# Seven products for two gate and up pairs in each of seven FFNs of a two-block transformer kernel

## The reference

```
def swiglu(x, w_gate, w_up, w_down):
    return (jax.nn.silu(x @ w_gate) * (x @ w_up)) @ w_down      # 1024 -> 2816 -> 1024
```

## Time and profile before

| | us |
|---|---|
| median of 3 runs (2456.72 to 2456.9) | 2456.76 |
| span of the profiled execution | 2455.0 |
| TensorE busy | 2426.3 |
| VectorE busy | 1559.7 |
| ScalarE busy | 1183.0 |
| GpSimd busy | 205.5 |

### The profile page before, as it was taken

One profiled execution on the slowest core, in us unless ns is written; L12 is line 12 of the kernel. 1 busy time (PEld: TensorE's weight loads), 2 busy tenths in 40 slices (PEclk: granted clock), 3 DMA queues, 4 the chain that ended last, 5 costly groups with the idle time before them and its releaser, 6 DMA issues.

```text
span 2455.0 us, 30703 instructions
## 1 busy us (share of the span) xinstructions
PE 2426.3 (99%) x12690; PEld 2069.7 (84%) x12690; DVE 1559.7 (64%) x1629; ACT 1183.0 (48%) x1276; POOL 205.5 (8%) x358
## 2 busy tenths in 40 slices
PE   8999999999999999999999999999999999999998
PEld 6889998888889988888889878888888898788887
DVE  6555876655656776565558657656665677577664
ACT  5435544434437544444435664544344356644442
POOL 0100200100100101101100010011011000100010
PEclk9999999999999999999999999999999999999999
DMA  8755447657654447657664445476576454454762
GB/s 334 238 209 189 156 165 246 227 209 237 236 204 181 164 148 272 227 205 259 227 214 174 161 154 206 180 262 231 202 256 231 172 184 152 150 208 159 256 232 101
DMA packets 82547, 504.42 MB, mean 205 GB/s; under 512 B 11608, under 2 KB 12760, under 8 KB 30184
## 3 DMA queue, kind: packets, MB, share of 16 engines
q1 hardware_dynamic: 61488, 433.23, 49.2%
q0 software_dynamic: 19744, 67.65, 8.6%
q10 hardware_dynamic: 1176, 1.58, 0.4%
HBM read 476.72 MB, written 25.69 MB: 205 GB/s over the span
## 4 chain that ended last, share of the span: by engine, by line
PE 91%; DVE 5%; ACT 3%; issue 1%; DMA 1%; SPq 0%; POOL 0%; DVEq 0%; POOLq 0%; ACTq 0%
PE acc L615 24%; PE acc L616 24%; PE acc L617 24%; PE acc L583 4%; PE acc L584 4%; PE acc L585 4%; DVE w_lo L516 2%; PE aux L799 1%; ACT w_hi L508 1%; DMA raw<-in_w 1%; ACT tmp L1484 1%; PE stat L633 1%; PE bc L633 0%; PE aux L1170 0%; PE aux L981 0%
## 5 line engine op out<-in xcount | busy, mean ns | idle before, releaser
L516 DVE TENSOR_TENSOR w_lo<-raw,w_hi 128x2048 fp32r<-128x2048 f32 (+1 forms) x417 | 934.3, 2244 | 672.3 <-ACT w_hi L508 671.5
L508 ACT ACTIVATE w_hi<-raw 128x2048 fp32r<-128x2048 f32 (+1 forms) x417 | 782.8, 1880 | 624.2 <-PE acc L617 594.0
L615 PE MATMUL acc<-w_hi,x_hi 128*128 128x512 f32 (+1 forms) x1848 | 720.4, 390 | 3.1 <-DVE x_lo L1736 2.1
L617 PE MATMUL acc<-w_lo,x_hi 128*128 128x512 f32 (+1 forms) x1848 | 715.6, 387 | 0.0
L616 PE MATMUL acc<-w_hi,x_lo 128*128 128x512 f32 (+1 forms) x1848 | 715.5, 387 | 0.0
L615 PEld LDWEIGHTS acc<-w_hi,x_hi 128*128 128x128 f32 x1848 | 347.1, 188 | 77.8 <-issue 6.1
L617 PEld LDWEIGHTS acc<-w_lo,x_hi 128*128 128x128 f32 x1848 | 347.0, 188 | 71.3
L616 PEld LDWEIGHTS acc<-w_hi,x_lo 128*128 128x128 f32 x1848 | 347.2, 188 | 70.4 <-issue 1.0
L615 PE MATMUL acc<-w_hi,h_parts 128*128 128x512 f32 x704 | 274.5, 390 | 0.0
L617 PE MATMUL acc<-w_lo,h_parts 128*128 128x512 f32 x704 | 273.9, 389 | 0.0
L616 PE MATMUL acc<-w_hi,h_parts 128*128 128x512 f32 x704 | 273.9, 389 | 0.0
(11 more groups left out here) (396 smaller groups left out, 2229.3 us busy)
## 6 DMA issues: line engine op xcount, KB each, us to landing
raw<-in_w SPq DMA_DIRECT2D x399, 1024.0 KB, 4.8
squares<-tmp POOLq DMA_DIRECT2D x40, 512.0 KB, 2.9
tmp<-squares POOLq DMA_DIRECT2D x160, 128.0 KB, 4.5
raw<-in_w SPq DMA_DIRECT2D x18, 512.0 KB, 3.6
tmp<-in_norm_gb POOLq DMA_DIRECT2D x8, 1024.0 KB, 5.4
tmp<-in_norm_gb POOLq DMA_DIRECT2D x6, 512.0 KB, 3.7
tmp<-in_gate_rows POOLq DMA_DIRECT2D x12, 256.0 KB, 3.1
squares<-tmp POOLq DMA_DIRECT2D x8, 256.0 KB, 2.3
```

The lines of the kernel that those rows point to most:

```text
L508: nc.scalar.activation(w_hi[:, slot, 0:kind], raw[:, slot, 0:kind], ACT.Copy).then_inc(hi_done, 1)
L516: nc.vector.tensor_tensor(w_lo[:, slot, 0:kind], raw[:, slot, 0:kind], w_hi[:, slot, 0:kind].bitcast(F32), ALU.subtract).then_inc(lo_done, 1)
L615: nc.tensor.matmul(out, vh, wh, start=first and k == 0, stop=False)
L617: last = nc.tensor.matmul(out, vh, wl, start=False, stop=last_k and k == nk - 1)
```

## The change

In the seven FFNs other than the first, blocks 1 and 3 are computed in another way. With the input cut in two halves of tokens and two halves of rows (X11, X12, X21, X22) and the weights cut in gate and up, rows 0 to 511 and 512 to 1023 (B11, B21 are gate, B12, B22 are up), the four output quarters come from seven products instead of eight. Four of them take sums of quarters of X (computed by GpSimd in `x_sums`, once for an FFN, and split by `sum_high` and `sum_low`), and four take sums of the weights (T1 to T4), which VectorE writes into raw slots of the ring. A product is 12 matmuls of 512 columns.

A chunk number now stands for a product or for a chunk of an ordinary block. A group covers one block of seven products and the ordinary block behind it, in this order: T1, B11, B22, gate 0, T2, B21, T3, gate 1, T4, up 0, up 1. The two groups of an FFN begin at c0+4 and c0+15. T2, T3 and T4 have no load (`None` in GROUP). T2 = T1 + B22 and T3 = T2 - B11 are written after the split of B22 (`middle_sums`), T4 = T2 + B21 after that of B21 (`last_sum`); T1 = B12 + B11 is written over the loaded B12 (`first_sum`). The loads of B21 and of up 0 wait for T3 and T4. The products gather in the banks `bc` and `aux`, from which ScalarE and VectorE copy and combine them (`kept`).

Small things ride along: some semaphores are merged, and a table (HOT) lies elsewhere in `tmp`. The diff, cut to its core:

```diff
-FFN = [WIDE] * (UP_CHUNKS + 5) + [HALF] * 2 + [WIDE] * 5
-SUBS = ["ffn", "mix1", "ffn"] * 2 + ["ffn", "mix2", "cross", "ffn"] * 2
-KINDS = {"ffn": FFN, "mix1": MIX1, "mix2": MIX2, "cross": CROSS}
-TILES = {"ffn": 26, "mix1": 30, "mix2": 46, "cross": 10}
+FFN0 = [WIDE] * (UP_CHUNKS + 5) + [HALF] * 2 + [WIDE] * 5
+FFN = [WIDE] * (UP_CHUNKS + 6 + 5) + [HALF] * 2 + [WIDE] * 5
...
+B11, B21, B12, B22 = range(4)
+GROUP = (B12, B11, B22, 4 + B11, None, B21, None, 4 + B21, None, 4 + B12, 4 + B22)
+G_T1, G_B11, G_B22, G_GATE0, G_T2, G_B21, G_T3, G_GATE1, G_T4, G_UP0, G_UP1 = range(11)
+GROUPS = ((1, 4), (3, 15))
...
+            if sub == "ffn" and j in (4, 15):
+                n = len(GROUP)
+                out += [None if at is None else place[kind] + at for at in GROUP]
+                place[kind] += 8
...
+            if c in sums:
+                act.wait_ge(weight_sum, sums.index(c) + 1)
+            else:
+                act.wait_ge(loaded[slot], 16 * landings[c])
...
+                if place is None:
+                    continue
+                if c - G_B21 in group_at:
+                    sp.wait_ge(weight_sum, 4 * group_at.index(c - G_B21) + 3)
+                elif c - G_UP0 in group_at:
+                    sp.wait_ge(weight_sum, 4 * group_at.index(c - G_UP0) + 4)
+                elif c >= RING:
                     sp.wait_ge(lo_done, c - RING + 1)
...
+                def product(c, bank, v_hi, v_lo, first):
+                    chunk_ready(c)
+                    for k in range(4):
+                        wh, wl = wblock(c % RING, k, 512)
+                        nc.tensor.matmul(bank, v_hi[:, k], wh, start=first and k == 0, stop=False, skip_group_check=True)
+                        nc.tensor.matmul(bank, v_lo[:, k], wh, start=False, stop=False, skip_group_check=True)
+                        last = nc.tensor.matmul(bank, v_hi[:, k], wl, start=False, stop=k == 3, skip_group_check=True)
+                    last.then_inc(chunk_done, 1)
+                def group(g, b, tile):
+                    a_, b_, e_ = aux[:, 0, :], aux[:, 1, :], bc[:, :]
+                    x11, x12, _, x22 = ((x_hi[:, k, at], x_lo[:, k, at]) for k, at in X_AT)
+                    s1, s3, s2, s4 = zip(SUM_HI, SUM_LO)
+                    pe.wait_ge(sum_parts, 4 * (f - 1) + 1)
+                    if b:
+                        pe.wait_ge(outs_ready, 3 * b - 2)
+                    product(g + G_T1, e_, *s1, True)
+                    if b:
+                        pe.wait_ge(kept_silu, 2 * b)
+                    product(g + G_B11, b_, *x11, True)
+                    pe.wait_ge(sum_parts, 4 * f)
+                    pe.wait_ge(kept_copied, 3 * b + 1)
+                    product(g + G_B22, e_, *s4, False)
+                    both(g + G_GATE0, tile, 0)
+                    pe.wait_ge(kept_copied, 3 * b + 2)
+                    product(g + G_T2, b_, *s2, False)
+                    if b:
+                        pe.wait_ge(outs_ready, 3 * b - 1)
+                    product(g + G_B21, a_, *x12, True)
+                    pe.wait_ge(kept_copied, 3 * b + 3)
+                    product(g + G_T3, b_, *s3, False)
+                    both(g + G_GATE1, tile, 1)
+                    pe.wait_ge(outs_ready, 3 * b + 3)
+                    product(g + G_T4, b_, *x22, False)
+                    both(g + G_UP0, tile + 2, 0)
+                    both(g + G_UP1, tile + 2, 1)
...
+                def sum_high(q):
+                    act.wait_ge(sum_ready, 4 * (f - 1) + q + 1)
+                    nc.scalar.activation(SUM_HI[q], XQ4[SUM_AT[q]], ACT.Copy).then_inc(sum_hi, 1)
+                def kept(g, b, i):
+                    ended_chunk(act, g + G_T1)
+                    act.wait_ge(sum_parts, 4 * f)
+                    if i > 1:
+                        act.wait_ge(hid_ready, 12 * f + 2 * (i - 2) + 2)
+                    nc.scalar.activation(Q5B, bc[:, :], ACT.Copy).then_inc(kept_copied, 1)
+                    ahead.to(g + 4)
+                    ended_chunk(act, g + G_B11)
+                    nc.scalar.activation(P1B, aux[:, 1, :], ACT.Copy).then_inc(kept_copied, 1)
+                    ahead.to(g + 5)
                     if i > 1:
                         hid_high(i - 2)
-                    silu(i, 0)
-                    silu(i, 1)
-                    for j in range(1, 4 if i < 5 else 2):
-                        if s == 6 and i == 2 and j == 1:
-                            bias_copy()
-                        ahead.to(c0 + 4 * i + j + 4)
+                    ahead.to(g + 7)
+                    ended_chunk(act, g + G_T2)
+                    nc.scalar.activation(UB, aux[:, 1, :], ACT.Copy).then_inc(kept_copied, 1)
+                    ahead.to(g + 9)
+                    act.wait_ge(outs_ready, 3 * b + 2)
+                    nc.scalar.activation(P1B, P1B, ACT.Silu).then_inc(kept_silu, 1)
+                    ahead.to(g + 10)
+                    hid_high(i - 1)
+                    silu(i + 1, 0)
+                    silu(i + 1, 1)
+                    ahead.to(g + 11)
+                    ended_chunk(act, g + G_T4)
+                    nc.scalar.activation(G1B, aux[:, 1, :], ACT.Silu).then_inc(kept_silu, 1)
+                    ahead.to(g + 14)
+                def ups():
+                    if s == 0:
+                        ahead.to(c0 + 4)
+                    silu(0, 0)
+                    if s:
+                        sum_high(0)
+                    ahead.to(c0 + 4)
+                    if s:
+                        for q in range(1, 4):
+                            sum_high(q)
...
+                def sum_low(q):
+                    dve.wait_ge(sum_hi, 4 * (f - 1) + q + 1)
+                    V_.tensor_tensor(SUM_LO[q], XQ4[SUM_AT[q]], SUM_HI[q].bitcast(F32), ALU.subtract).then_inc(sum_parts, 1)
+                def kept_times(i, tt, gates_, ups_, ready):
+                    n = 12 * f + 2 * i + tt
+                    dve.wait_ge(squares_ready, n - 1)
+                    dve.wait_ge(*ready)
+                    V_.tensor_tensor(HID[:, tt], gates_, ups_, ALU.mult).then_inc(hid_ready, 1)
+                    dve.wait_ge(hid_ready, n + 1)
+                def slot(c):
+                    return raw[:, c % RING, 0:WIDE]
+                def first_sum(g):
+                    for c in (g + G_T1, g + G_B11):
+                        dve.wait_ge(loaded[c % RING], 16 * landings[c])
+                    V_.tensor_tensor(slot(g + G_T1), slot(g + G_T1), slot(g + G_B11), ALU.add).then_inc(weight_sum, 1)
+                def middle_sums(g):
+                    b = group_at.index(g)
+                    dve.wait_ge(lo_done, g + G_B22 + 1)
+                    V_.tensor_tensor(slot(g + G_T2), slot(g + G_T1), slot(g + G_B22), ALU.add).then_inc(weight_sum, 1)
+                    dve.wait_ge(weight_sum, 4 * b + 2)
+                    V_.tensor_tensor(slot(g + G_T3), slot(g + G_T2), slot(g + G_B11), ALU.subtract).then_inc(weight_sum, 1)
+                def last_sum(g):
+                    dve.wait_ge(lo_done, g + G_B21 + 1)
+                    V_.tensor_tensor(slot(g + G_T4), slot(g + G_T2), slot(g + G_B21), ALU.add).then_inc(weight_sum, 1)
+                def kept(g, b, i):
+                    ahead.to(g + 4)
                     if i > 1:
                         hid_low(i - 2)
-                    if i < 5:
+                    ahead.to(g + 5)
+                    last_sum(g)
+                    ahead.to(g + 7)
+                    dve.wait_ge(kept_copied, 3 * b + 3)
+                    V_.tensor_tensor(UB, bc[:, :], UB, ALU.subtract).then_inc(outs_ready, 1)
+                    ahead.to(g + 8)
+                    ended_chunk(dve, g + G_B21)
+                    dve.wait_ge(kept_copied, 3 * b + 2)
+                    V_.tensor_tensor(P1B, P1B, aux[:, 0, :], ALU.add).then_inc(outs_ready, 1)
+                    ahead.to(g + 9)
+                    ended_chunk(dve, g + G_T3)
+                    dve.wait_ge(kept_copied, 3 * b + 1)
+                    V_.tensor_tensor(Q5B, Q5B, aux[:, 1, :], ALU.subtract).then_inc(outs_ready, 1)
+                    dve.wait_ge(outs_ready, 3 * b + 1)
+                    kept_times(i, 0, P1B, UB, (kept_silu, 2 * b + 1))
+                    ahead.to(g + 10)
+                    hid_low(i - 1)
+                    if i == 1:
+                        first_sum(g + 11)
+                    ahead.to(g + 11)
+                    dve.wait_ge(outs_ready, 3 * b + 3)
+                    kept_times(i, 1, G1B, Q5B, (kept_silu, 2 * b + 2))
+                    turn_squares(i)
+                    ahead.to(g + 13)
+                    if i == 1:
+                        middle_sums(g + 11)
+                    times(i + 1, 0)
+                    times(i + 1, 1)
+                    turn_squares(i + 1)
+                    ahead.to(g + 14)
+                def ups():
+                    if s == 0:
+                        ahead.to(c0 + 6)
+                    else:
```

(96 more changed lines are left out.)

174 lines of the change are left out of this document (100 added, 74 removed).

## The result

The changed kernel takes 2538.55 us (median of 4 executions, 2531.94 to 2542.56) against 2456.83 before: a ratio of 1.033, 95% interval 1.0314 to 1.0346. The forecast was 2540. The profiled execution is the fastest of the four at 2531.94, with a span of 2530.2, so sums over the trace fall some 7 us short of the median.

A forecast was written before the change was run, and what follows sets the result against it. It took the kernel to be bound by TensorE's number of matmuls. The span of 2455.0 plus 121 us of stalls less 38 saved gave 2538; the median standing 1.8 above the span, it predicted 2540, range 2466 to 2562.

The forecast's parts named there:

- The saving: Two blocks in seven FFNs take seven products for eight: 14 products of 2.72 us removed from TensorE, 38.1 us.
- VectorE's added work: In a group, 11 splits and four weight sums (33.8 us) plus short operations (8.2 us): 42 us against TensorE's 40.8.
- The sums of X: At the FFN's head, GpSimd's eight operations at 1.4 us each, 11.6 us with waits, plus 4.7 us of VectorE conflicts.
- the walk: Step-by-step timing of one FFN's engines from its head: 17.2 us of stall an FFN, 50 in 100 as told.
- X+13.2: Predicted time of the last sum of X, counted in us from X, the end of chunk c0.
- The wait before B11: In the first group, TensorE has done T1 and stalls 7.4 us until B11 is split.
- The wait before the first gate 0: From B22 to gate 0 VectorE needs 10.9 us, TensorE's two products 5.4: a stall of 5.5 us.
- The wait before the second gate 0: In group two VectorE ends gate 0's split at X+73.7, TensorE wants it at X+70.2: a stall of 3.5 us.
- The two small waits after it: In group two VectorE's backlog shows twice more, before T3 and T4: 0.3 and 0.5 us.
- the rival that the clock falls too: Stalls bring TensorE's slow clock back, mostly hidden: up to 1.9 us an FFN, 13 in all, 2553; 10 in 100.
- The rival with the X sums in time: GpSimd near its lower bound, no lock: no stall before B11, 3.0 before gate 0; 2470; 13 in 100.
- The rival of a faster kernel: VectorE runs its chain without gaps, stall under 5.44 us an FFN: 2457, or 2419 with none; 7 in 100.

The follow-up runs named there:

- experiment 3: Changed kernel with both GpSimd's sums of X cut to 32 of 512 elements and VectorE's weight sums cut to 128 of 2048 columns: 2418.69 us, ratio 0.9843.
- Experiment 2: Changed kernel with VectorE's four weight sums of a group cut to 128 of 2048 columns: 2468.36 us, ratio 1.0047.
- experiment 5: Changed kernel, whole, with 23 dummy matmuls behind T1 and 22 ahead of the first gate 0 in each of seven FFNs: 2541.16 us, ratio 1.0343.
- experiment 1: Changed kernel with GpSimd's eight sums of X cut to 32 of 512 elements: 2479.14 us, ratio 1.009.
- experiment 7: Changed kernel with only the first group: block 1 as seven products, blocks 3 and 4 ordinary: 2532.0 us, ratio 1.0306.
- experiment 8: Changed kernel with one later group (block 2 as seven products), X-sum splits behind block 0, gate 0 split ahead of the multiplications: 2448.34 us, ratio 0.9965.
- experiment 9: Kernel of experiment 8 with the split of T3 moved ahead of the sum for T4 on VectorE: 2458.12 us, ratio 1.0005.

## Why the prediction was right

The forecast of 2540 met 2538.55. By its steps:

- **The saving.** 38.1 us: experiment 3 gives it to within 0.1.
- **VectorE's added work.** A weight sum takes 2.29 us, as the row over `tmp` said, at the pitch of 2.25 to 2.3.
- **The sums of X.** GpSimd was free where the walk had it. Two terms were over-sized. The operation is the first: 1.29 us against the 1.4 that I took between 0.74 and 1.49. From 376.60 to 390.89 the eight take 14.3 us; alone they would be 10.3, so some 4.0 are conflicts with VectorE and short gaps, against 4.7 in the walk. The last sum is ready at X+11.2 in place of X+13.2 (X is 379.7). Experiment 2 ties the first conflict to `first_sum`; that the others come from VectorE too is read from operations that run at the same time.
- **The wait before B11.** 5.7 us (40.8 in seven) against 7.4, short by about that term.
- **The wait before the first gate 0.** 3.3 us against 5.5. The step that failed is that I let B11 run at full clock in the sum. VectorE's chain was right: the splits of B11 and B22 begin at 393.87, and from the end of the first, at about 396.1, to the end of gate 0's, 407.2, it is 11.1 us against 10.9 in the walk. What TensorE did in between was longer: B11 and B22 take 7.8 us (396.22 to 404.02) where the walk has 5.4. Only B11 is slow, 10 of its 12 matmuls; B22 has the pitch of 0.23.
- **The wait before the second gate 0.** 2.3 us against 3.5 at the clock that it had, and 3.9 with the clock kept up till there (experiment 5). The difference of 1.6 us is about what the eight slow matmuls of the first gate 0 cost (1.7). The two small waits after it (0.8 us an FFN) did not come.
- **The clock.** It fell in all seven waits before B11, at six of the seven before the first gate 0 and at one of those before the second. So the rival that the clock falls too came true, and with it the reason that it would cost little: up to the second gate 0 it took the place of waits. The sum of the waits was therefore too large (121 against 81), and what I had in no term of the sum made up 32, some 27 of them slow matmuls. From the table load ahead of the first silu of the second FFN to that of the third (374.84 and 566.63) it is 191.8 us, against 181.4 before (374.71 and 556.10): 15.8 us lost beside the 5.4 saved, against 17.2 in the walk.

So the mechanism and the total were right, and the split between waiting and slow matmuls was not. That the total came out within 2 us is partly luck. The wait before B11 was over-sized by 1.7 us an FFN, 12 in all, so that the same walk with the measured length would have given 2528. The measured median is 10.6 above that, and the sum has no term for it. What fills the gap is not shown for the median. The profiled execution, at 2531.94, is the fastest of the four and has a clock of 0.984, where the others have 0.979 to 0.983. Falls behind the second gate 0, one in its profile, could do it: seven of them cost 13 us in experiment 5.

The rival with the X sums in time is what experiment 1 built: 2479 for its 2470. It had the wait before the first gate 0 nearly right (3.0 against 3.16) and no term for the slow matmuls. The rival of a faster kernel had the right point, 5.44 us an FFN, and nothing that computes the whole result reached it with two groups. I did not try the conflict of GpSimd and VectorE with the same work on both and no overlap, so its price rests on the lengths of single operations.

Three slips in the working change nothing: seven times 17.2 is 120.4 and not 120.6; between the waits of 9.2 and 2.1 us TensorE has one kind of 3.1 (for L2286, twice); and 2578 is 5.4 us an FFN over 2540, where 5.4 more over 2553 would be 2591.

## What to carry to other kernels

When a change takes work off the engine that bounds a kernel and puts it on another, add up the second engine's work for the stretch that gets shorter, not for the kernel: VectorE was 64% busy over the span of the kernel before and had 42 us to do in a group of 40.8. Then walk the chain at the head of the stretch, where inputs come late; the same transformation, once an FFN and behind an ordinary block, and with the order on VectorE changed in four places, gained 0.6% where twice and at the head it lost 3.3%. A single group cost 75 us at the head (experiment 7) and gained 8.5 us behind an ordinary block (experiment 8), which had another order on VectorE as well; the two were not tried apart. An order written by hand carries loads with it: moving one sum by one place delayed a load, a split and a release of a bank, and cost more than the wait that it removed.

## What the runs showed of the hardware that I had not expected

Short waits bring TensorE's granted clock to its lower level. Behind the wait of 5.7 us the matmuls have a pitch of 0.43 us (396.81 to 397.24 in the changed kernel), as at 1.2 GHz, and of 0.23 again from 400.64. The length of the wait alone doesn't tell. The clock fell at six of seven waits of 3.16 us in experiment 1, at one of seven before the second gate 0 in the changed kernel (at 2.3 us, and not at 3.5), and at three of seven of 1.7 to 1.9 us in experiment 9.

What a fall costs depends on what comes next. Where VectorE set the time of a later chunk, it came out of the wait there (experiments 1 and 5). Where no such wait followed, it was paid: about 14 us in experiment 2, and 13 behind the second gate 0 in experiment 5.

GpSimd's tensor_tensor over 512 elements takes 1.29 us alone and up to 3.34 beside a VectorE split.
